# Opening of a hybrid S5/convolution/PEER step on one core: when the first tile's rows, roots and scores are loaded, how many query slabs precede the first slots, and the x transposes in two parts

## The reference

```
xn = RMSNorm(x);  z = xn @ w_in -> u_ssm (512), conv GLU input (1024), gate logits (2048)
A  = GLU(gelu(S5 scan of u_ssm));   B = swish(LN(depthwise conv(GLU))) @ w_conv_out
x2 = x + (sigmoid(gA)*A + sigmoid(gB)*B) @ w_out
q  = RMSNorm(x2) @ w_q           # 8 heads, 2 x 128 per head
s1, s2 = q halves @ keys1, keys2 # 128 scores each; top 16 of each, top 16 of the 256 sums
e  = 16 expert numbers per head and row;  g = softmax(top sums)
y  = x2 + sum over the 128 (head, expert): g * gelu(u_tab[e] . xn2) * v_tab[e]
output RMSNorm(y), plus the final states of scan and convolution
```

## Time and profile before

| | |
|---|---|
| median of 3 runs | 3489.51 us (3487.99 to 3494.52) |
| the profiled execution's own time | 3491.98 us |
| its span, first to last instruction | 3489.9 us |
| busy: PE / DVE / POOL / ACT | 3148.8 / 2409.2 / 1417.6 / 1214.4 us |
| moved by DMA | 1336.40 MB, of it 1140.92 MB by the gathers |
| granted TensorE clock, mean | 0.976 of full speed |

### The profile page before, as it was taken

One profiled execution on the slowest core, in us unless ns is written; L12 is line 12 of the kernel. 1 busy time (PEld: TensorE's weight loads), 2 busy tenths in 40 slices (PEclk: granted clock), 3 DMA queues, 4 the chain that ended last, 5 costly groups with the idle time before them and its releaser, 6 DMA issues.

```text
span 3489.9 us, 33576 instructions
## 1 busy us (share of the span) xinstructions
PE 3148.8 (90%) x10016; PEld 1794.4 (51%) x10016; DVE 2409.2 (69%) x5463; ACT 1214.4 (35%) x4060; POOL 1417.6 (41%) x1240
## 2 busy tenths in 40 slices
PE   7998999999999999999999999999999777777776
PEld 6776555555655455555655555555555222322222
DVE  7824599776656699776656699777656666676674
ACT  4222443343333334343333343333333333333332
POOL 1201455433334355443334355343333444444443
PEclk9999999999999999999999999999999999999999
DMA  4257999999999999999999999999999999999998
GB/s 134 96 175 275 380 381 410 418 419 419 418 398 412 395 386 407 418 410 418 416 398 415 393 385 406 419 415 419 418 406 405 420 420 420 402 420 408 419 398 344
DMA packets 232069, 1336.40 MB, mean 383 GB/s; under 512 B 27664, under 2 KB 49296, under 8 KB 92624
## 3 DMA queue, kind: packets, MB, share of 16 engines
q0 software_dynamic: 156672, 1140.92, 79.7%
q1 hardware_dynamic: 62992, 179.96, 13.9%
q10 hardware_dynamic: 12224, 13.38, 1.1%
HBM read 1310.93 MB, written 23.23 MB: 382 GB/s over the span
## 4 chain that ended last, share of the span: by engine, by line
PE 53%; DMA 25%; DVE 10%; issue 5%; ACT 5%; POOL 2%; SPq 0%; POOLq 0%; DVEq 0%; ACTq 0%
PE ps_acc L760 29%; DMA rows<-in_experts,idx 24%; PE ps_a L596 13%; DVE rows L1375 4%; PE ps_a L671 4%; PE ps_v L596 3%; POOL rows L1521 2%; DVE va L1225 1%; PE ps_a L698 1%; ACT coef L918 1%; ACT uy L817 1%; ACT diag L922 1%; PE ps_y L638 1%; PE ps_a L675 1%; PE ps_v L682 0%
## 5 line engine op out<-in xcount | busy, mean ns | idle before, releaser
L760 PE MATMUL ps_acc<-rows,diag 128*128 128x512 f32 x4352 | 2020.8, 613 | 282.4 <-ACT diag L922 279.7
L1521 POOL DMA_INDIRECT rows<-in_experts,idx x1088 | 1280.1, 1177 | 1788.5 <-PE ps_acc L760 1468.6
L1375 DVE CUSTOM_DVE_ANT_0 rows<-rows,xn 128x1024 f32<-128x1024 f32 x1088 | 1328.4, 1232 | 839.1 <-DMA rows<-in_experts,idx 832.3
L760 PEld LDWEIGHTS ps_acc<-rows,diag 128*128 128x128 f32 x4352 | 824.3, 195 | 1335.4 <-issue 865.1
L915 ACT ACTIVATE act_v<-dots 128x2 f32<-128x2 f32 x544 | 110.6, 203 | 1894.1 <-DVE dots L1375 1891.1
L922 ACT ACTIVATE diag<-pk,coef 128x128 f32<-128x128 f32 x1088 | 377.2, 394 | 17.7
L596 PE MATMUL ps_a<-xnT,ring 128*128 128x272 f32 x1536 | 370.3, 396 | 0.9 <-ACT xnT L805 0.7
L596 PEld LDWEIGHTS ps_a<-xnT,ring 128*128 128x128 f32 x1536 | 293.4, 192 | 91.8 <-issue 34.8
L918 ACT ACTIVATE coef<-act_v,soft 128x1 f32<-128x1 f32 x1088 | 261.4, 287 | 17.9
L596 PE MATMUL ps_a<-gates,ring 128*128 128x272 f32 x1024 | 247.5, 395 | 15.2 <-ACT sig L892 14.4
L1225 DVE SCALAR_TENSOR_TENSOR va<-va,pk 128x302 f32<-128x302 f32 x480 | 250.2, 584 | 2.7
(11 more groups left out here) (226 smaller groups left out, 2001.0 us busy)
## 6 DMA issues: line engine op xcount, KB each, us to landing
ring<-in_slabs SPq DMA_DIRECT2D x256, 512.0 KB, 7.8
rows<-in_experts,idx POOLq DMA_INDIRECT x1088, 12.6
ring<-made_slabs SPq DMA_DIRECT2D x24, 512.0 KB, 9.3
sc<-score_rows SPq DMA_DIRECT2D x68, 128.0 KB, 10.2
score_rows<-gp ACTq DMA_DIRECT2D x32, 256.0 KB, 9.6
xt<-in_x_prompt SPq DMA_DIRECT2D x4, 1024.0 KB, 13.1
x_rows<-xt ACTq DMA_DIRECT2D x4, 1024.0 KB, 12.3
x2t<-x_rows SPq DMA_DIRECT2D x8, 512.0 KB, 11.7
```

The lines of the kernel that those rows point to most:

```text
L760: ins = pe.matmul(ps_acc[:, h, :], diag[:, slot, :], rows[:, slot, D + h * 512:D + (h + 1) * 512], start=first, stop=False, skip_group_che ...
L1375: ins = dve.tensor_tensor_reduce(rows[:, slot, 0:D], rows[:, slot, 0:D], xn[:, :], 1.0, 0.0, ALU.mult, ALU.add, dots[:, s:s + 1])
L1521: pool.indirect_dma_start(out=rows[:, slot, :], out_offset=None, in_=experts, in_offset=bass.IndirectOffsetOnAxis(ap=idx[:, a, k:k + 1], a ...
```

## The change

`OPEN` goes from 59 to 62 and `SKEW` from 4 to 3: halves 59 to 61 (q[9] to q[11], score[8] to score[10]) join the part without slots, the first six halves of the turns finish `OPENING`, and every group of `STEADY` begins one turn earlier. `load_rows` is split: SP loads x2 at the half of `ms2` (55) once it is stored, and the roots (`load_roots`) two halves later, one after `rs`. The two loads of scores stand one half earlier. DVE does `choose(0, 0)` and `choose(0, 1)` ahead of its half 55, in front of the mean of x2's squares. `xn` becomes two parts of four transposes, at halves 0 and 1, and in `STEADY` cq[0] moves from half 1 to half 2.

```diff
--- before.py
+++ after.py
@@ -64,7 +64,7 @@
 HALVES = 2 * TURNS
 PIECES = ("xn", "u", "cq", "cp", "s", "y", "gate", "glu", "mean", "var", "cout", "out", "rows", "q", "score")
 SLAB_OF = {"u": 0, "cq": S_CONV, "cp": S_CONV + 1, "gate": S_GATE, "glu": S_GLU, "cout": S_COUT, "out": S_OUT, "q": S_Q}
-A_TILES = {"xn": DT, "u": 1, "cq": 1, "gate": 1, "glu": 1, "out": 1, "q": 1, "score": 1}
+A_TILES = {"xn": DT // 2, "u": 1, "cq": 1, "gate": 1, "glu": 1, "out": 1, "q": 1, "score": 1}
 V_TILES = {"cp": 1, "s": 2, "glu": 1, "mean": 1, "var": 1, "cout": 2, "rows": 2}
 A_BANKS, V_BANKS = 2, 3
 
@@ -107,7 +107,7 @@
 
 
 OPENING = Plan(
-    {"xn": [0], "u": [1, 2, 3, 4], "cq": [5, 7, 9, 11], "cp": [6, 8, 10, 12],
+    {"xn": [0, 1], "u": [1, 2, 3, 4], "cq": [5, 7, 9, 11], "cp": [6, 8, 10, 12],
      "s": [10, 12, 14, 16], "y": [15, 18, 21, 24],
      "gate": [13 + m for m in range(13)] + [34 + m for m in range(3)], "glu": [26 + j for j in range(DT)],
      "mean": [29], "var": [32], "cout": [37, 38, 39, 40], "out": [42 + j for j in range(DT)],
@@ -120,7 +120,7 @@
      "cout": [38, 39, 40, 41], "rows": [52, 53, 54], "sq": [54], "ms2": [55], "rs": [56],
      "load_x": [59], "sq_next": [63], "ms_next": [64], "norm_next": [65]}, False, 0)
 STEADY = Plan(
-    {"xn": [0], "u": [9, 11, 21, 23], "cq": [1, 5, 13, 17], "cp": [3, 7, 15, 19],
+    {"xn": [0, 1], "u": [9, 11, 21, 23], "cq": [2, 5, 13, 17], "cp": [3, 7, 15, 19],
      "s": [12, 16, 24, 28], "y": [20, 24, 32, 36],
      "gate": [25 + 2 * m for m in range(10)] + [44, 54] + [61 + 2 * m for m in range(4)],
      "glu": [45 + 2 * j for j in range(DT)],
@@ -139,8 +139,8 @@
 SLABS_0, SLABS_G = len(OPENING.slabs), len(STEADY.slabs)
 SLABS = SLABS_0 + (GROUPS - 1) * SLABS_G
 
-SKEW = 4
-OPEN = 59
+SKEW = 3
+OPEN = 62
 ALL_TURNS = TILES * TPAIRS * PTURNS + SPAIRS * PTURNS
 LAST_PAIR = TILES * TPAIRS + SPAIRS - 1
 
@@ -459,6 +459,8 @@
             def load_rows(t):
                 rows_free(t)
                 sp.dma_start(x2t[:, t % 2, :], x2_t[t]).then_inc(x2_in, 16)
+
+            def load_roots(t):
                 sp.dma_start(rst[:, t % 2, :], rs_t[t]).then_inc(rs_in, 16)
 
             def beside(number):
@@ -496,13 +498,15 @@
                 mix(h, 0)
 
                 for b in range(2):
-                    if h == OPENING.pe["score"][2 * b + 1] + 2:
+                    if h == OPENING.pe["score"][2 * b + 1] + 1:
                         sp.wait_ge(score_out[b], 32)
                         load_scores(0, b)
-                if h == OPENING.pe["q"][8]:
+                if h == OPENING.other["ms2"][0]:
                     sp.wait_ge(rows_out, 32)
+                    load_rows(0)
+                if h == OPENING.other["rs"][0] + 1:
                     sp.wait_ge(rs_out, 48)
-                    load_rows(0)
+                    load_roots(0)
             sp.wait_ge(score_used, 1)
             sp.wait_ge(score_out[0], 64)
             load_scores(1, 0)
@@ -512,6 +516,7 @@
                 beside(2 * turn)
                 if k == 3 and g < GROUPS:
                     load_rows(2 * g + 1)
+                    load_roots(2 * g + 1)
                 if k == 1 and g < GROUPS:
                     sp.wait_ge(score_out[1], 128 * g + 64)
                     pass_wait()
@@ -529,6 +534,7 @@
                     sp.wait_ge(rs_out, 48 * (g + 2))
                     pass_wait()
                     load_rows(2 * g + 2)
+                    load_roots(2 * g + 2)
                 if turn == TILES * TPAIRS * PTURNS - 6:
                     rows_free(TILES)
                     for f in range(2):
@@ -596,15 +602,16 @@
                     last = pe.matmul(out[:, 0:N], w, rhs[:, k, :], start=(k == 0), stop=(k == kt - 1))
                 return last
 
-            def to_channels(n0, g):
+            def to_channels(n0, part, g):
 
                 pe.wait_ge(xh_ready, g + 1)
-                for k in range(DT):
-                    out = a_tile(n0 + k)
+                for k in range(DT // 2 * part, DT // 2 * (part + 1)):
+                    out = a_tile(n0 + k % (DT // 2))
                     for t in range(2):
                         pe.transpose(out[:, t * P:(t + 1) * P], xh[t][:, k * P:(k + 1) * P], eye)
                     pe.transpose(out[:, NP:N], xh[2][:, k * P:(k + 1) * P], eye[0:NS, 0:NS]).then_inc(a_ready, 1)
-                a_emptied(n0 + DT - 1)
+                if part == 1:
+                    a_emptied(n0 + DT // 2 - 1)
 
             def states(t, g):
 
@@ -701,8 +708,8 @@
 
             def mix(h, g):
                 at = plan(g).at
-                for _ in at("xn", h):
-                    to_channels(a_at(g, "xn"), g)
+                for part in at("xn", h):
+                    to_channels(a_at(g, "xn", part), part, g)
                 for m in at("u", h):
                     to_a("u", m, xnT[:, :, :], g)
                 for j in at("cq", h):
@@ -798,9 +805,9 @@
                 act.activation(va[:, D:2 * D], xt[:, 1, :], ACT.Square, accum_out=ssq[:, 1:2])
                 act.activation(xh[2], xt[0:NS, 2, :], ACT.Square, accum_out=ssq[0:NS, 2:3]).then_inc(sq_x, 1)
 
-            def to_channels(n0, name, g):
-                for k in range(DT):
-                    src, out = ready(n0 + k), by_step(xnT[:, k, :])
+            def to_channels(n0, part, name):
+                for k in range(DT // 2 * part, DT // 2 * (part + 1)):
+                    src, out = ready(n0 + k % (DT // 2)), by_step(xnT[:, k, :])
                     act.activation(out[:, :, 0:KP], in_time(src[:, 0:NP]), ACT.Copy, scale=par(name)[:, k:k + 1])
                     act.activation(out[:, :, KP:NK], in_time(src[:, NP:N]), ACT.Copy,
                                    scale=par(name)[:, k:k + 1]).then_inc(a_done, 1)
@@ -840,8 +847,8 @@
                 def at(piece, h):
                     return plan(g).at(piece, h - plan(g).lag)
 
-                for _ in plan(g).at("xn", h):
-                    to_channels(a_at(g, "xn"), "norm_mix", g)
+                for part in plan(g).at("xn", h):
+                    to_channels(a_at(g, "xn", part), part, "norm_mix")
                 for m in at("u", h):
                     cross(uS[:, m, :], ready(a_at(g, "u", m)), ACT.Copy, False).then_inc(a_done, 1)
                 for j in at("cq", h):
@@ -1417,8 +1424,11 @@
             for h in range(OPEN):
                 if h == OPENING.pe["s"][0]:
                     setup_lags()
+                if h == OPENING.other["ms2"][0]:
+                    for r in range(2):
+                        choose(0, r)
                 mix(h, 0)
-            for r in range(PTURNS):
+            for r in range(2, PTURNS):
                 choose(0, r)
             dve.wait_ge(norms_in, 16)
             for turn in range(ALL_TURNS):
```

## The result

Median 3465.85 us (4 runs, 3464.63 to 3468.11) against 3490.76 us before (4 runs, 3487.99 to 3494.52): ratio 0.9928, 95% interval 0.9913 to 0.9943. The profiled execution took 3465.22 us, its span is 3463.1 us, 26.8 less than before.

What follows compares the result with a forecast made beforehand. After the opening the speed of the gathers on the DMA engines was taken as the bound. Opening 5.9 plus transposes 2.0 made 7.9 us off 3491.98, 3484.1, and a median 2.5 lower: 3481.6 us, range 3474 to 3490.

Steps and rivals of the forecast that it cites:

- By the DMA's count: Opening: bytes stay the same, so only idle DMA time can be filled; 5.9 us gained, ends 4.6 and 8.1.
- The smaller of two limits counts: Opening: of PE's 12.6 us and the DMA engines' 5.9 us, the forecast takes 5.9.
- PE's count: Opening: PE's work up to group 1's transposes, less two halves of slots at the end, gains 12.6 us.
- PE's count holds: Rival, chance 0.13: in the opening the DMA engines have slack their share hides; 12.6 + 2.0, giving 3475 us.
- Transposes in two parts: Around groups 2 and 3: two slots free their buffers between the parts; 2.0 us taken, between 0 and 7.2.
- the shift of the steady mixer: Steady groups: mixer one turn earlier against the `choose` steps, work in each stretch the same; no gain in the sum.
- the slower rival: Chance 0.07: in stretches where DVE is busy, the shifted mixer raises DMA idle time by 16 us, giving 3498 us.
- The lead: Opening rival, chance 0.30: q[13]'s slab lands late, PE stands 4 us, first slots at 333.5; 3487 us.
- not earlier: Opening rival, chance 0.03: first scores take 14.75 us to load, first gather is late by 5; 3490 us.

Runs made afterwards that it cites:

- two_part_xn: Kernel before with the transposes of x in two parts and cq[0] one half later, nothing else; 3482.24 us against 3491.43.
- q_only: Kernel before with `OPEN` 62 instead of 59 alone, loads late and `SKEW` 4 as before; ratio 0.9993.
- best_skew3: Changed kernel with the second pair's first scores loaded at half 58 and group 1's x at half 58 instead of 59; 3478.6 us.
- four_skew4: Changed kernel with the transposes of x in four parts, first cq and cp products later, and `SKEW` 4 instead of 3; 3468.7 us, ratio 0.9928.

## Why the prediction was wrong, point by point

**Right.** First gather 298.8 (298.63 measured), first slots 329.5 (330.48), group 1's transposes 360.7 (362.70). The scores took 3.9 us for the 5.1 taken. The mean of squares ran at 291.90, and ACT stored the roots at 294.04 with nothing late behind it. The roots landed by 315.59, inside the bounds of 306 to 316, and PE went on without a gap to the first slots. What moving cq[0] costs by itself no run shows.

**First failed step: "By the DMA's count" and "The smaller of two limits counts".** That is where 5.9 came from, against a measured 11.5; PE's count of 12.6 was right to 1.1 us. The rule of the smaller limit is not what fell: the DMA limit was read from the wrong column. Idle time was (1.02 - share) x length, which takes 1.02 for full speed whatever it moves. The row itself spoke against it: 0.93 beside 349 GB/s, where 0.93/1.02 of 418 would be 381. By GB/s the stretch from 331.45 holds 51.85 x (1 - 349/418) = 8.6 us, not 4.7; and the 280 to 400 us windows above give 12.1. The forecast's own sum redone by bytes is 0.71 x 4.2 = 3.0, the 1.25 of x2 and 8.6, less the same 1 and 1.2: 10.6, near the 11.5. The rival "PE's count holds", at 0.13, named just this slack; what I held against it, that the stretch holds small stores, fell as well. DMA packets from 340 to 360 us, before:

```profile
DMA packets 1620, 7.87 MB, mean 394 GB/s; under 512 B 182, under 2 KB 582, under 8 KB 838
```

And after, more small packets and more bytes:

```profile
DMA packets 1879, 8.34 MB, mean 417 GB/s; under 512 B 311, under 2 KB 718, under 8 KB 1109
```

I read the issuing rule of the Trainium skill (DMA: Bandwidth & Descriptors, Issuing engines are not separate DMA queues) as putting 12.6 out of reach. It says that all issuers share the same 16 engines, not that these were full, and at 349 GB/s against 418 they were not.

**Second failed step: "Transposes in two parts", 2.0, "nearer to none, since the sum of PE's work there is the same".** Alone they gave 9.8 (two_part_xn). The upper bound of 7.2 had the same fault of the share: 60 x (1 - 381/418) is 5.3 us a group, 10.6 for two, and 9.6 of the 10.7 idle us went. And the reason was wrong: the sum of PE's work did stay the same, but POOL's gathers stood for 12.2 us in a row while PE freed no slot, and for 9.1 with two parts.

**Third: the shift of the steady mixer at nothing.** Alone it is worth nothing in the steady part, as taken. With two parts it adds some 7 us in the stretch beside DVE, where the slower rival had looked for a loss. The prediction had no term for parts that work together.

**The rivals.** The lead was not eaten by q[13]'s slab, which landed in time; another load, the second pair's scores, which the prediction does not name, took 1.2 us of PE (and 7.41 in q_only), and best_skew3 shows the rival's price when it does happen, some 12 us at the first slots. The slower rival and "not earlier" did not happen.

**Open.** Why the stretch 100 to 180 us behind the transposes gains only where `SKEW` 3 (or 2, once of twice) meets split transposes. The runs place it, rule out the transposes' own hold, and show POOL's passes over the scan's states as one thing that the gathers stand behind there; why these cost less after the change is not shown. Open too is what four parts add to two.

## What to carry to other kernels

Count idle DMA time by bytes moved against the best stretch of the same kernel, not by busy share. Where a gather ring feeds an engine, look for that engine's longest hold without freeing a buffer, not for the sum of its extra work, and split that hold even where the sum stays; then count the idle time well past it, for it can come back further on, as with four parts here. When loads are reordered ahead of a tight consumer, count for each queue what now goes out before it: one half in x's load turned a gain of 27 us into 16.

## What was not expected of the hardware

- A DMA share of 1.00 to 1.02 moved 394 to 397 GB/s between 320 and 360 us before the change; after it, 1.02 moved 417 to 420 between 340 and 380.
- Behind the gathers, size said little of a load's time: the 1 KB of roots took 14.75 us before and 12.0 after; 128 KB of scores took 3.9 us at 284, ahead of the first gather, 16.6 at 321, 22.3 in four_skew4 and 25.3 in q_only.
- Waits of PE cost more than their length here. Behind a stop of PE of 8.98 us the next product took 6.41 instead of 3.93 us; behind one of 6.05 eight slot matmuls took 6.07 instead of 3.70 us. The granted clock was 0.62 both times (335 to 342 us in best_skew3, 347.5 to 354 in four_skew4), between its levels of 1.2 and 2.4 GHz.
